# Block two's choosing steps spread over its three attentions, and one wait for each map's memory

## The reference

```python
def dsa_attention(q, k, v, iq, ik, iw, t5_table):
...
        logits = jnp.einsum('bqhd,bsd->bqhs', iqb, ikf) * (IDX_DIM ** -0.5)
        score = jnp.einsum('bqhs,bqh->bqs', jax.nn.relu(logits), iwb * (IDX_HEADS ** -0.5))
        score = jnp.where(admissible[None], score, -jnp.inf)
        _, idx = lax.top_k(score, k_sel)
...
        p = softmax_f32(s, v.dtype)
...

def hybrid_layer_2(x, mem, ...):
...
    ya = spatial_gating(...)
    yb = chunk_band_attention(heads(bq), heads(bk), heads(bv), b_rel)
    yc = dsa_attention(heads(cq), heads(ck), heads(cv), iq, ik, iw, t5_table)
    ym = memory_attention(heads(mq), km, vm)
    mixed = jnp.concatenate([ya * jax.nn.silu(a_g), yb * jax.nn.silu(bg),
                             yc * jax.nn.silu(cg), ym * jax.nn.silu(mg)], axis=-1)
    y = mixed @ w_out + b_out
```

## Time and profile before

| what | value |
|---|---|
| median of 3 runs | 3619.6 us (3612.26 to 3623.09) |
| the profiled execution | 3616.24 us, span 3614.4 us |
| PE busy | 3141.3 us (87%) |
| DVE busy | 2060.6 us (57%) |
| ACT busy | 1197.4 us (33%) |
| POOL busy | 436.6 us (12%) |

### The profile page before, as it was taken

How to read it: one execution, slowest core, us unless ns; L and a number is a source line. 1 busy time by engine, 2 the same in 40 slices (tenths; PEclk the granted TensorE clock), 3 DMA queues, 4 the chain that set the end, 5 groups by cost and what they waited for, 6 DMA issues and landing times. The chain is left out here.

```text
span 3614.4 us, 37560 instructions
## 1 busy us (share of the span) xinstructions
PE 3141.3 (87%) x14208; PEld 2393.5 (66%) x14208; DVE 2060.6 (57%) x3113; ACT 1197.4 (33%) x2280; POOL 436.6 (12%) x407
## 2 busy tenths in 40 slices
PE   6999889886788879899997762989976989999999
PEld 5787667664677768677885552444554468888887
DVE  5112544487688835839886876549865334444444
ACT  2211231586566632234225651000264011112111
POOL 2000002344011100222340031010000000000000
PEclk9999999997899999999998986999988999999999
DMA  6323125433633334341462410411011011111111
GB/s 215 134 72 101 42 83 189 140 119 103 165 94 94 88 143 149 99 101 53 129 201 85 129 59 31 161 69 56 14 35 62 0 47 47 47 47 47 47 58 59
DMA packets 189934, 326.63 MB, mean 90 GB/s; under 512 B 16242, under 2 KB 110610, under 8 KB 189754
## 3 DMA queue, kind: packets, MB, share of 16 engines
q1 hardware_dynamic: 168602, 250.29, 22.7%
q0 software_dynamic: 21152, 73.94, 5.7%
HBM read 233.71 MB, written 89.16 MB: 89 GB/s over the span
## 5 line engine op out<-in xcount | busy, mean ns | idle before, releaser
L215 PE MATMUL banks<-b3h4a_hi,b3mlpw_part 128*128 128x512 f32 x1024 | 319.8, 391 | 6.8 <-DVE b3mlpw_part L3277 6.8
L215 PE MATMUL banks<-b3mlpw_part,b3mlp_acthi 128*128 128x512 f32 x1024 | 315.2, 389 | 0.0
L215 PE MATMUL banks<-b1ln_w,b_hThi 128*128 128x512 f32 x768 | 239.5, 393 | 0.0
L215 PEld LDWEIGHTS banks<-b3h4a_hi,b3mlpw_part 128*128 128x128 f32 x1024 | 193.7, 189 | 47.5 <-issue 7.1
L215 PEld LDWEIGHTS banks<-b3mlpw_part,b3mlp_acthi 128*128 128x128 f32 x1024 | 192.2, 188 | 39.9
L3324 DVE TENSOR_TENSOR b3out_x<-b3out_x,banks 128x1024 f32<-128x1024 f32 x128 | 154.8, 1219 | 111.6 <-PE banks L215 111.6
L215 PE MATMUL banks<-b3out_lo,b3mlpw_part 128*128 128x512 f32 x512 | 200.4, 391 | 0.0
L215 PE MATMUL banks<-b3mlpw_part,b3mlp_actlo 128*128 128x512 f32 x512 | 199.2, 389 | 0.0
L508 PE MATMUL banks<-b_hThi,b1item_hi 128*128 128x512 f32 x464 | 196.2, 423 | 3.4 <-DVE b1item_lo L497 3.1
L3294 ACT ACTIVATE b3mlp_relu<-banks 128x1024 f32<-128x1024 f32 x32 | 32.9, 1029 | 499.5 <-PE banks L215 499.5
L508 PE MATMUL banks<-b_hThi,b1item_lo 128*128 128x512 f32 x464 | 183.4, 395 | 0.0
(11 more groups left out here) (417 smaller groups left out, 6716.8 us busy)
## 6 DMA issues: line engine op xcount, KB each, us to landing
qk_spill<-b1scan_qk SPq DMA_DIRECT2D x64, 256.0 KB, 2.8
b1att_k<-qk_spill SPq DMA_DIRECT2D x64, 256.0 KB, 8.2
b1out_ws<-in_w_out SPq DMA_DIRECT2D x16, 1024.0 KB, 5.0
b3mlpw_stage<-in_w_mlp_up SPq DMA_DIRECT2D x16, 1024.0 KB, 5.3
b3mlpw_stage<-in_w_mlp_down SPq DMA_DIRECT2D x16, 1024.0 KB, 4.9
b2h_stage<-in_w_in SPq DMA_DIRECT2D x30, 512.0 KB, 4.1
b1item_stage<-in_w_in SPq DMA_DIRECT2D x29, 512.0 KB, 4.9
b1ln_stage<-in_w_in SPq DMA_DIRECT2D x12, 1024.0 KB, 6.8
```

The costliest lines, as they stand in the source:

```text
L215: last = pe.matmul(out, x, y, start=i == 0, stop=i == n - 1)
```

## The change

The credit of a round becomes 1.7 in the band and memory attentions and 1.3 in the sparse one. The four maps and the second mask are put on the ring rows in the order of those rows' last use, and instead of the waits ahead of all rounds, the shift of each of the units 0 to 3 waits for its own row, and POOL's first mask for the fifth. The sixth row, whose store is the last one, is under none of them.

```diff
--- before.py
+++ after.py
@@ -2610,15 +2610,14 @@
 def dve_attend(K, top):
     v, S, vs, C = K.v, K.S, K.vs, K.attend
 
-    def rows_free():
-
-        for n, part in USES2[-RING2:]:
-            if ITEMS2[n][0] in ("bv", "dv") and part == 0:
-                v.wait_ge(S["p1_turned"], misc2(K, ("t",) + ITEMS2[n]) + 1)
-            else:
-                v.wait_ge(*K.stores[("pass", n, part)])
-
-    rows_free()
+    def row_free(i):
+
+        n, part = USES2[-RING2:][i]
+        if ITEMS2[n][0] in ("bv", "dv") and part == 0:
+            v.wait_ge(S["p1_turned"], misc2(K, ("t",) + ITEMS2[n]) + 1)
+        else:
+            v.wait_ge(*K.stores[("pass", n, part)])
+
     for r in range(ALL_UNITS + 6):
         u = r
         if u < ALL_UNITS:
@@ -2626,7 +2625,7 @@
             if A.sel and h == 0:
                 while t in K.sel and t not in K.chosen:
                     top.step()
-            top.pump(1.0, ST - 1)
+            top.pump({"b": 1.7, "m": 1.7, "d": 1.3}[A.kind], ST - 1)
         u = r - 1
         if 0 <= u < ALL_UNITS:
             s = K.stat[u % 12]
@@ -2652,6 +2651,8 @@
                 bias = C.mask[n % 2][:, 0:width]
             if u >= 4:
                 v.wait_ge(S["at_turned"], u - 3)
+            else:
+                row_free(u)
             v.wait_ge(S["at_sc"], u + 1)
             if bias is None:
                 v.tensor_scalar(e, bank, -1.0, 3e38, ALU.mult, ALU.min, accum_out=s[:, 0:1]).then_inc(S["at_shift"], 1)
@@ -2681,6 +2682,8 @@
                     g.wait_ge(S["chosen"], t - 1)
                 if n < 4:
                     g.wait_ge(S["at_edge"], 4 + h + 1)
+                if n == 0:
+                    g.wait_ge(*K.stores[("pass",) + USES2[-2]]) if USES2[-2][1] else g.wait_ge(S["p1_turned"], len(MISC2))
                 if n >= 2:
                     g.wait_ge(S["at_shift"], A.u0 + 8 + n - 1)
                 g.tensor_tensor(C.mask[n % 2][:, 0:(t + 1) * P], A.bias(h, t), K.sel[t], ALU.add).then_inc(S["at_mask"], 1)
@@ -3477,8 +3480,9 @@
     C = K.attend = Part()
     a = Space(nc, "b2turn", mem0 + 36 * 1024, late0)
     C.turned = a.several("turned", 3, [P, ST, P])
-    a = Space(nc, "b2maps", ring0, TOP)
-    C.maps, C.mask = a.several("map", 4, [P, S_LEN]), [mask, a.take("mask", [P, S_LEN])]
+    ring = [stage_at(n, part) for n, part in USES2[-RING2:]]
+    C.maps = [Space(nc, f"b2map{i}", ring0 + 4 * S_LEN * ring[i], TOP).take("map", [P, S_LEN]) for i in range(4)]
+    C.mask = [mask, Space(nc, "b2mask", ring0 + 4 * S_LEN * ring[4], TOP).take("mask", [P, S_LEN])]
     C.outT = Space(nc, "b2outT", mid0 + 12 * 1024, ring0).take("outT", [P, 2, S_LEN])
 
     first = lambda t: max(0, t - 4)
```

## The result

The changed kernel takes 3581.43 us (median of 4 runs, 3576.74 to 3584.39), the kernel before 3620.26 us beside it (3612.26 to 3623.09). The ratio is 0.9892, with a 95% interval of 0.9875 to 0.9908: 1.1% faster, about 39 us. The time is 8 us under the 3589 of the forecast and inside its range. The profiled execution has a span of 3574.9 us.

The account below looks back on a forecast made before the run. The prediction took DVE to set the pace, its idle time being what counts. Terms -10.6 - 11.1 - 6.6 - 4.2 + 3.5 = -29.0 us, counted from 3618, gave 3589 us, range 3579 to 3604.

Parts of the forecast that it names:

- the start: Ahead of the band attention: first shift at 1915.1 instead of 1925.7 us, no wait for the last `dv_spill` store, -10.6 us.
- band: idle filled: Band attention: ten added steps fill DVE's waits, -9.1 us for ACT and -2.0 for PE, together -11.1 us.
- memory: idle filled: Memory attention: nine added steps and a mask fill DVE's waits for ACT, PE and a store, together -6.6 us.
- sparse: idle filled: Sparse attention up to unit 91: four steps come in, a mask goes; DVE's waits fall, together -4.2 us.
- the run ahead of unit 92: Before unit 92: 23 steps, 59.3 us, leave and come back elsewhere; no term of its own.
- PE's clock: Lower PE clock in the attentions costs 2.5 us in the memory and 1 us in the band attention, +3.5 us.
- DVE sets the pace, so only its idle time counts: Attentions from 1910 us on: DVE sets the pace and its busy time stays the same, so its idle time counts.
- the first rival: PE's clock stays low in much of the memory attention, costing 12 us there; time 3600 to 3603 us, chance 0.15.
- my own sign for that rival: Memory attention: PE's clock at 0.5 for half of it would mean a low clock costing 12 us there.
- the steps hide nothing: In all rounds, a step costs its full length wherever it is; gain only 12.5 us, 3605 us, chance 0.05.
- the start gains nothing: Ahead of the band attention, another load or store replaces the last store's wait; gain 18.4 us, 3600 us, chance 0.05.
- The slower one: PE at 1.2 GHz becomes the pace of all three attentions: +20 us, 3638 us, chance 0.02.

Follow-up runs that it names:

- the second profile: The unaltered changed kernel measured and profiled once more: 3582.41 us, ratio 0.9890 to the kernel before.
- the spread alone: The kernel before with only the new credits of a round, all its waits ahead of the rounds kept: 3593.90 us, ratio 0.9934.
- the start alone: The changed kernel with the credit of a round back at 1.0, so only the maps' places and own waits are new: 3610.22 us, ratio 0.9977.

## Why the prediction was right, and where a term was off

| term of the sum | forecast, us | measured, us |
|---|---|---|
| the start | -10.6 | -10.5 |
| band: idle filled, against 23.2 of steps | -11.1 | 12.2 - 23.2 = -11.0 |
| memory: idle filled, against 24.1 of entries | -6.6 | 16.7 - 24.1 = -7.4 |
| sparse: idle filled, against 12.1 of entries | -4.2 | 4.1 - 12.1 = -8.0 |
| the run ahead of unit 92, 23 steps | -59.3, back elsewhere | -59.4 |
| PE's clock | +3.5 | none in the first profile, perhaps 1.1 in the second |
| sum | -29.0 | -36.7, and -35.1 in the second profile |

The measured column is from the table of lengths. The entries' lengths are those of the forecast: a step of block 6 lasts 2.32 us and one of block 7 2.58, and in the memory attention 15 entries of block 6 become 14 steps, the mask and 10 steps of block 7; in the sparse one 9 steps, a mask and 3 steps of block 7 become 16 of block 7.

**What held.** The step "DVE sets the pace, so only its idle time counts" carried the whole: the kernel with the step behind the reciprocal does the same work in the same rounds and loses 48 us. The start was right in its size, its end (PE's scores) and in that nothing else took its place. The waits for ACT left in the band and memory attentions are 4.5 and 4.6 us, where I had 5.0 and 4.6, because waits in rounds of known width can be counted.

**What was luck.** That the band attention comes out within 0.1 us. DVE's waits there fell by 8.6 us for ACT where I had 9.1 (the 14.1 of the earlier trace rows hold one wait of the next stage) and by 1.3 for PE where I had 2.0, 9.9 us in all. The other 1.1 us is no idle time that was filled: ten added steps cost that much less than the 2.32 us each that I counted (more on it in the last section). In the memory attention it is the same, 6.1 us of waits and 1.3 of this, and there it shows as 7.4 against 6.6. And the time lies inside the range only by its allowance of 4 us for the median: the gain of the attentions, 36.7 and 35.1 us, is above the 34.5 at which the forecast's own bounds end.

**What failed.** Two steps, together nearly all of the 8 us.

First, the +3.5 of PE's clock, with its "at the lower level, 1.2 GHz, the same work takes up to 2.99 us". The clock did fall, as the first rival had it: a mean of 0.74 is about half of the memory attention at 0.5, which was my own sign for that rival. But it cost nothing there. I had doubled 1.49 us, PE's mean busy time of a unit in the stage. PE's work for one unit, before, at a granted clock of 1.00:

```profile
2056.00:2060.00 4.00, 2.55 (x19) 1.00 0.00 1
2058.91 0.65 PE L184 MATMUL banks<-b2turn_turned,b2mem_mv 128*64 128x128 f32 x4 [1.45 <-ACT b2turn_turned L2607]
2059.49 0.51 PE L184 MATMUL banks<-b2mem_mk,b2mem_mq 128*128 128x256 f32 x2
2059.84 0.38 PE L206 MATMUL banks<-fixed_eye,b2maps_map 128*128 128x128 f32 x2
```

and in the changed kernel, at 0.50:

```profile
2060.00:2064.00 4.00, 3.24 (x13) 0.50 0.00 0
2062.91 1.12 PE L184 MATMUL banks<-b2turn_turned,b2mem_mv 128*64 128x128 f32 x4 [0.76 <-ACT b2turn_turned L2607]
2063.96 0.80 PE L184 MATMUL banks<-b2mem_mk,b2mem_mq 128*128 128x256 f32 x2
2064.55 0.63 PE L206 MATMUL banks<-fixed_eye,b2map_map 128*128 128x128 f32 x2
...
2076.00:2080.00 4.00, 4.00 (x16) 0.50 0.00 0
2080.00:2084.00 4.00, 1.52 (x10) 0.93 0.01 2
```

From the start of the first to the end of the last that is 1.31 us and 2.27 us. So the unit was shorter than the 1.49 I started from (that mean holds the wider units that PE still has from the band attention, when it is nearly full up to 2012 us), and it grew 1.73 times, not 2. At 1.2 GHz it takes 2.27 us, which is 0.28 less than the mean round of 2.55 us (81.7/32). My argument against the rival, that PE fills up at 1.2 GHz and gets its clock back, did happen: PE works without a pause from 2073.55 to 2080.2 us, and the next slice has 0.93. But the clock falls again in the slice behind it (0.50), and none of this matters where the stage is DVE's. The first rival had the right event with the wrong price. The section "A second HAM failure mode: psum-queue depth-cycling" of the page "TensorE: Matmul & The Clock Gate" in the Trainium skill has the clock going back and forth, and the trace agrees (0.50 to 1.00 in slices of 4 us between 2024 and 2120 us). That this costs throughput is not borne out in this stage, where another engine sets the pace.

Second, the sparse attention's -4.2. DVE's waits there fell by 12.6 - 9.4 = 3.2 us for ACT where I had 1.8, by 2.4 for the store where I had 1.9, by 0.9 for PE where I had 0.5, and POOL's 1.3 us of waits for masks went, which I had left standing:

```profile
DVE b2maps_map L2659 <- POOL b2maps_mask L2686: 1.3, 2, 0.8
```

For ACT I took the width of the round's own unit; the wait is for the unit before, and three of the twelve rounds follow a gate, which covers part of it. POOL's masks are in time with the spread alone, too, while with the start alone 0.8 us of the wait stays, so it is mostly DVE's longer rounds that do it: an engine that is late before is on time when the pace-setting one has more to do.

**The rivals.** That the steps hide nothing and that the start gains nothing are out by the trace. The slower one needed PE to be full at 1.2 GHz throughout, and PE had room, 2.27 of 2.55 us in the memory attention.

## What to carry to other kernels

Work that can run at any time belongs where its engine would wait for another one's answer, and the exact place counts: one instruction further on, the same steps in the same rounds hid nothing of the wait for ACT, 48 us in all. When one engine paces a stage, add up its waits by round; in two attentions they gave the waits for ACT that were left within 0.5 us. Before doubling an engine's time for a lower clock, find the same work in the trace at that clock. One wait for many buffers ahead of a loop costs as much as the latest of them, even if that buffer is used last or not at all.

## What was not expected of the hardware

PE's time for a unit of small products (two of 256 columns, two turns and four products of 128 columns) rose from 1.31 us at a granted clock of 1.00 to 2.27 at 0.50, a factor of 1.73 rather than 2. In the memory attention its price in time was nil, at means of 0.71 to 0.87 against 1.00.

DVE's total busy time fell by 2.6 us, from 2060.6 to 2058.0, though it does the same instructions. In the timelines a step behind a shift starts together with the shift's 0.08 us read of the accumulator (both at 1963.40 above), so the two overlap where in a round without a step they don't; 23 steps of 0.08 would be 1.8 us of it. With the start alone the total is 2060.6 as before and with the spread alone 2057.9, so the fall comes with the moved steps. That the overlap is the whole cause was not tested.
